# Two scores before the last block of queries: a barrier removed at the start of a banded attention

## The reference, cut to what matters

```python
p = h @ w_in
q, k, v, mq = jnp.split(p, [Q_W, Q_W + KV_W, Q_W + 2 * KV_W], axis=-1)
...
scores = jnp.einsum('bnqhgd,bnkhd->bnhgqk', qb, kb) * (ATTN_HEAD_DIM ** -0.5)
scores = jnp.where(mask, scores, NEG)            # |key - query| <= 128
m = jnp.maximum(jnp.max(scores, axis=-1, keepdims=True), s)   # s: a sink for each head
p = jnp.exp(scores - m)
probs = p / (jnp.sum(p, axis=-1, keepdims=True) + jnp.exp(s - m))
out = jnp.einsum('bnhgqk,bnkhd->bnqhgd', probs.astype(v.dtype), vb)
...
mo = memory_attention(mq, mk, mv)
x = x + jnp.concatenate([mixed, mo], axis=-1) @ w_out[l]
```

## Time and profile before

| | |
|---|---|
| median of 3 runs | 3200.7 us (3200.01 to 3201.22) |
| the profiled execution | 3196.59 us |
| its span, first to last instruction | 3194.8 us |
| mean granted TensorE clock | 0.989 |
| TensorE, busy | 3080.3 us, 96% |
| VectorE, busy | 1696.2 us, 53% |
| ScalarE, busy | 1105.6 us, 35% |
| GpSimd, busy | 89.9 us, 3% |

### The profile page before, as it was taken

One profiled execution on the slowest core, in us unless ns is written; L12 is line 12 of the kernel. 1 busy time (PEld: TensorE's weight loads), 2 busy tenths in 40 slices (PEclk: granted clock), 3 DMA queues, 4 the chain that ended last, 5 costly groups with the idle time before them and its releaser, 6 DMA issues. The chain is left out here.

```text
span 3194.8 us, 34615 instructions
## 1 busy us (share of the span) xinstructions
PE 3080.3 (96%) x14262; PEld 2387.1 (75%) x14272; DVE 1696.2 (53%) x2173; ACT 1105.6 (35%) x1723; POOL 89.9 (3%) x70
## 2 busy tenths in 40 slices
PE   8999999999999999999999999999999999999888
PEld 7885567788888888777777888888887687666566
DVE  7737854544444433589854633333333734656575
ACT  4215632311111111387732311111111515776552
POOL 0004510000000000000000000000000000000000
PEclk9999999999999999999999999999999999999999
DMA  4320011122222211211131111111111131000213
GB/s 148 114 94 1 1 73 34 53 80 66 67 79 73 73 47 47 86 47 47 54 124 34 47 47 46 47 53 46 47 47 46 53 124 35 20 21 20 93 39 121
DMA packets 54510, 190.96 MB, mean 60 GB/s; under 512 B 6288, under 2 KB 6672, under 8 KB 54224
## 3 DMA queue, kind: packets, MB, share of 16 engines
q1 hardware_dynamic: 54352, 188.74, 18.0%
HBM read 172.73 MB, written 14.68 MB: 59 GB/s over the span
## 5 line engine op out<-in xcount | busy, mean ns | idle before, releaser
L285 PE MATMUL PS<-H,wsp 128*128 128x512 f32 x6864 | 1613.8, 394 | 38.7 <-DVE wsp L141 16.5
L285 PEld LDWEIGHTS PS<-H,wsp 128*128 128x128 f32 x6864 | 1290.6, 189 | 347.1 <-issue 40.1
L285 PE MATMUL PS<-p,wsp 128*128 128x512 f32 (+1 forms) x3840 | 895.2, 393 | 20.7 <-DVE p L141 20.7
L285 PEld LDWEIGHTS PS<-p,wsp 128*128 128x128 f32 x3840 | 711.3, 189 | 198.6 <-ACT wsp L138 21.5
L138 ACT ACTIVATE p<-p 128x1024 f32<-128x1024 f32 (+7 forms) x426 | 361.3, 872 | 861.6 <-DVE p L144 678.6
L138 ACT ACTIVATE wsp<-raw 128x1024 fp32r<-128x1024 f32 (+1 forms) x267 | 276.9, 1040 | 698.3 <-PE PS L285 490.9
L141 DVE TENSOR_TENSOR p<-p,PS 128x1024 f32<-128x1024 f32 (+2 forms) x232 | 244.4, 1054 | 496.5 <-PE PS L285 496.5
L141 DVE TENSOR_TENSOR wsp<-raw,wsp 128x1024 fp32r<-128x1024 f32 (+1 forms) x267 | 321.8, 1207 | 159.4 <-ACT wsp L138 152.4
L141 DVE TENSOR_TENSOR p<-PS,p 128x1024 f32<-128x1024 f32 (+2 forms) x116 | 131.0, 1130 | 371.8 <-PE PS L285 346.9
L141 DVE TENSOR_TENSOR p<-p 128x1024 fp32r<-128x1024 f32 (+5 forms) x239 | 239.6, 1010 | 114.8 <-ACT p L138 111.6
L285 PE MATMUL PS<-p 128*64 128x256 f32 (+9 forms) x1432 | 283.9, 464 | 12.7 <-ACT p L138 3.0
(11 more groups left out here) (70 smaller groups left out, 1051.4 us busy)
## 6 DMA issues: line engine op xcount, KB each, us to landing
raw<-in_in_dram SPq DMA_DIRECT2D x72, 512.0 KB, 3.5
raw<-in_dn_dram SPq DMA_DIRECT2D x65, 512.0 KB, 3.5
raw<-in_up_dram SPq DMA_DIRECT2D x64, 512.0 KB, 3.5
raw<-in_out_dram SPq DMA_DIRECT2D x42, 512.0 KB, 3.5
p<-in_ada_dram SPq DMA_DIRECT2D x24, 512.0 KB, 4.4
p<-in_x_dram SPq DMA_DIRECT2D x16, 512.0 KB, 7.3
raw<-in_kv_dram SPq DMA_DIRECT2D x16, 512.0 KB, 3.5
spill_dram<-p SPq DMA_DIRECT2D x16, 512.0 KB, 2.9
```

Of the source, the lines that this page charges most:

```text
L285: return pe(lambda e: e.matmul(o, l, r, start=start, stop=stop, **kw), *a)
```

## The change

The project call makes three blocks of memory queries in place of four. The fourth becomes a function `last_queries`, handed to `attention_units` as `lead`, which calls it after the second score group of unit 0 has been put into the lists; it sets the counter to 2 for it, so that it takes banks 4 and 5. The barrier is gone. In its place the scores and the values wait for the last operations of ScalarE, VectorE and GpSimd as they stood behind the third block (`heads_done`), the first users of `Pb` and of the transposed buffers wait for the same, and the second `Pb` buffer waits for the fourth block's eviction as well.

```diff
         def attention_units(units, nkmax, off, scale, sink=None, fill=None, fills=(), early=False, ahead=None, wide=None,
-                            pt_wait=None):
+                            pt_wait=None, lead=None):
...
-            pt_free, p_free = [pt_wait] * nT, [None, None]
+            pt_free, p_free = [pt_wait] * nT, [pt_wait, None]
...
                     pending = x
+                    if lead and u == 0 and j == J - 1:
+                        o = lead()
+                        p_free[1] = [*(pt_wait or ()), o]
                     for _ in range(fills[u] if fill and early else int(bool(fill) and fills[u] > 1)):
...
-        project("in0", 4, 8, Hk, by_R(MQ, R, box["r"], *kv_done))
-        Q.barrier()
+        project("in0", 3, 8, Hk, by_R(MQ, R, box["r"], *kv_done))
+
+        stage_end = heads_done = [x for x in (Q.last("act"), Q.last("dve"), Q.last("pool")) if x]
+
+        def last_queries():
+            pair[0] = 2
+            project("in0", 1, 8, Hk, lambda n, *a: by_R(MQ, R, box["r"], *kv_done)(3, *a))
+            return Q.last("dve")
...
-        attention_units(window_units(Qt, Kt, Vt, 2, 4, (-1, 0, 1), out0, bias0, sinkv0), 384, 80 * KB, 0.125, True)
+        attention_units(window_units(Qt, Kt, Vt, 2, 4, (-1, 0, 1), out0, bias0, sinkv0, heads_done, heads_done), 384, 80 * KB, 0.125, True,
+                        pt_wait=stage_end, lead=last_queries)
```

## The result

The changed kernel takes 3193.6 us (median of 12 runs, 3188.3 to 3194.6), the kernel before in the same session 3198.7 us (median of 12, 3192.3 to 3201.2). The ratio is 0.9982, with a 95% interval of 0.9973 to 0.9990: a gain of 0.18%, which is 5.8 us by the ratio, 5.2 us by the medians. The prediction had 3.8 us (0.12%), gave "no difference" 0.89, and put the forecast time 3.3 us above the measured one. The direction and the three places were right. The term of the start was mis-sized by more than its own length: 2.1 us expected, 4.97 in the two profiles.

What follows compares the result with a forecast made beforehand. TensorE, busy 96% of the span, was taken to bound the kernel. Start 2.1, first seam -1.2 and second seam 2.9 sum to 3.8 us, so 3200.7 becomes 3196.9 us; range 3193.0 to 3201.8.

Steps and rivals of the forecast that it cites:

- The term of the start: Start of the first banded attention: unit 2's second group turned at 261.95 instead of 264.06, a gain of 2.1 us.
- The wait in front of the scores: Before the first scores: the 1.48 us wait on an eviction stays, one block earlier, so scores start at 234.27.
- The fall of the clock over the held-back block: Over the held-back block's 48 matmuls: one 3.41 us stretch of half clock, costing 1.7 us.
- The rival that I gave 0.17: Clock stays up at the held-back block: start gains 3.8 us, whole gain 5.5 us, 3195.2 us; chance 0.17.
- The order on VectorE behind the block: Unit 0's second normalisation queues behind the block's eviction and unit 1's first maximum; its turn comes 3.8 us after eviction start.
- The pace behind it: First attention units behind the held-back block: two units take 9.6 us at full clock.
- What comes along: Weight split and 512 KB load accompanying the held-back block: hidden under its matmuls, cost nothing; uncovered some 2.4 us.
- The first seam: Rest of the first output projection: shifted bank pairs make a block wait for bank 7's eviction, loss 1.2 us.
- The second seam: Last output projection: shifted bank pairs remove its first block's 2.93 us idle wait for bank 7, gain 2.9 us.
- the rival without a fall: Clock stays at full rate at the held-back block: gain 5.5 us, giving 3195.2 us; chance 0.17.
- The noise: Whole-kernel timing: a measurement tells 0.2%, 6.4 us, from no change; "same" given 0.89.
- the rival of a second fall: Behind the held-back block the clock falls again, two units keep 11.51 us: gain 1.9 us, 3198.8 us; chance 0.16.

Runs made afterwards that it cites:

- Early waits: Changed kernel, but scores, values and first probabilities wait for the last operations before the first memory-query block, not behind the third; median 3190.4 us, ratio 0.9975 to the kernel before.
- before again: The unchanged kernel before, profiled a second time for its clock; one execution, 3196.6 us.
- the barrier alone: Kernel before without its barrier, four blocks and nothing moved, attention waiting for the last operations behind the fourth block; median 3196.5 us, ratio 0.9993.
- the first try without a gap: Kernel before without barrier, four blocks in pairs 0, 1, 2, 3, scores not waiting for these blocks, nothing held back; median 3200.7 us, ratio 1.0005.
- the rotation alone: Kernel before with four blocks and its barrier, but the bank-pair counter set to 3 behind the first attention; median 3195.5 us, ratio 0.9990.
- the second seam alone: Kernel before with one line more, the bank-pair counter set to 1 in front of the last output projection; median 3196.5 us, ratio 0.9983.

## Why the prediction was right or wrong

*The wait in front of the scores.* Right: it stays, 1.36 us, and belongs to the eviction. Early waits remove it.

*The fall of the clock over the held-back block.* Wrong, and it is the step that failed: "I don't think it does: what comes before the block is the same as what came before the fall." What came before was the same, what came after was not. In seven profiles with work held back (the changed kernel twice and five kernels made from it) the clock fell over the block in none; in two it fell behind it, for 3.4 us. In the seven with nothing held back it fell in the first units every time, for 3.4 to 13.7 us. The block's eviction started 46.8 us behind the mark, where the working has 46.7 without the fall and 48.4 with it. The rival that I gave 0.17 was the case. Without the fall, the term's own working (E + 13.4 for unit 2's second turn) gives 3.8 us. The length of 3.41 us that I took for the fall rested on a single stretch as well: near 1290 it was 3.4 us long in four of the 14 profiles, 6.8 in five and 10.2 in five.

What in the held-back work keeps the clock up stays open. The block does two things at once, it puts dense matmuls behind the scores and takes the wait for unit 0's exponentials away from TensorE, and no run has one without the other. Nor do the waits behind the block decide: they are the same 1.5 us in six of these seven profiles (0.56 and 0.96), and the clock fell there in two of the six.

*The order on VectorE behind the block.* Right to a tenth: unit 0's second group is turned 251.25 - 247.44 = 3.81 us after the eviction's start, 3.8 expected; the waits are 0.56 and 0.96 us, 0.6 and 0.9 expected.

*The pace behind it.* Mis-sized: I took 9.6 us for two units from the end of the attention, they take 8.4 at the start. That is another 1.2 us, and 3.8 + 1.2 = 5.0 is what was measured (4.97). The two pieces are not of the same shape after all. Inside the 9.59 us the eviction of a finished output stands on ScalarE and VectorE in front of the copies out of the turn's banks, and TensorE waits 0.65 and 0.34 us for these, 0.23 and 0.16 us later on; in the 8.38 us at the start no output is finished yet, and its waits are 0.27 and 0.25. These waits differ by 0.9 us of the 1.2; no run tests it. The row in the profile of before:

```profile
416.14 0.41 PE L538 MATMUL PS<-cf,p 128*128 128x128 f32 x2 [0.65 <-ACT p L138]
```

With a fall behind the block I took the old pace, 11.5 us, for two units; measured with a stretch of 3.4 us, 258.89 - 249.43 = 9.46.

*How much was the old clock?* The kernel before is not one case. With a stretch of 13.7 us unit 2's second turn comes at 64, with 3.4 or 6.8 us at 61.8 (in two kernels that are the same up to there); the changed kernel has it at 59 or 60. So the start gives 1.8 to 5.4 us, by the execution. I had read one profile of before as the kernel's fixed state.

*What comes along.* Right: the split is done at 240.9 under the block, and no wait for the load behind it shows on TensorE. The barrier's own price is 0.2 us of TensorE's time, and taking it out without moving anything makes no difference that the timing can tell.

*The first seam.* Right: 1.2 us expected, 1.04 measured, undone in each of the three kernels with the counter taken back.

*The second seam.* Right in the profile: 2.9 expected, 3.0 measured, and a version with that line alone keeps it. Too small as an expectation for a median: a fall of the clock followed the idle time there in three of the six profiles that have the gap (before again, the barrier alone, the first try without a gap), 1.4 us more each time (84.5 to 84.8 from there to the end, against 83.1), and in none of the eight that don't have it.

*The sum.* In the two profiles the three places give 6.9 us where the sum has 3.8: the start is 2.9 us better than its term, the seams together 0.3. The timing, 5.2 to 5.8 us, lies at the 5.5 of the rival without a fall, and that is partly luck: the rival's term for the start, 3.8 us, left out the faster pace, and the two profiles compare a start of before with a long fall to one of after with none, which is nearly the most that the four profiles of the two kernels allow (5.4 us).

*The noise.* Wrong, the second step that failed: "A measurement of this kernel tells 0.2%, 6.4 us, from no change", and with it the 0.89 for "no difference". The bound had no run or row behind it. Twelve runs of each kernel gave an interval of 0.9973 to 0.9990, 0.09% to either side, so a gain of 0.18%, inside my bound, can be told from none.

*The rule on transposes.* Part 4 of the Trainium skill's page "TensorE: Matmul & The Clock Gate" says that they do not count as activity like matmuls; by that rule the rival of a second fall would have been the case. It came in two of seven profiles, right where the first turns are, and cost 1.1 us there. So the trace agrees in part.

## What to carry to other kernels

Where a phase of dense matmuls is followed by one of short ones that starts with a chain over other engines, keep back a dense piece that doesn't depend on the chain and lay it behind the chain's first links; half a block was enough here. It paid twice, in the wait that it covered and in the clock, which fell in the first units of every profile without it and, for 3.4 us, in two of seven with it. A counter that deals out banks is part of the timing: before it is moved by an edit, list the places where rotating users follow fixed ones, and set it there on purpose; one such line was worth 3.0 us in the profile, the whole change 6.9. And take more than one profile of before where its clock is not at 1.00: a stretch of low clock may be 3.4 or 13.7 us long in the same program.

## What the runs showed of the hardware

*How long the low clock lasts.* With the same code up to there, its length in the first units was 13.7, 13.7, 6.8, 3.4 us (before twice, the rotation alone, the second seam alone). In the short, waiting work of these units TensorE stayed at 1.2 GHz while the records show it busy 12.46 of 13.65 us; but dense work is no warrant of a short stretch either: near 1290, in the midst of the MLP, it was 3.4, 6.8 or 10.2 us long.

```profile
243.75:246.10 2.35, 1.77 (x12) 1.00 0.00 0
246.10:259.75 13.65, 12.46 (x50) 0.50 0.00 1
```

*A fall in dense work.* Every profile has one near 1290 (1283 to 1295), where TensorE is shown busy without a break before it. I have no cause for it. It is the only one of its kind: each profile has 9 to 13 other stretches of low clock, and shortly before every one of those TensorE had been idle for 1.5 us or more in all. Idle time of that size did not always bring a fall, as the second seam and the end of the attention show.

*The first 200 us.* The mark comes at 198.4 to 199.0 us in the executions whose clock did not fall near 90, and at 200.1 to 201.0 in those where it did, for 3.4 us. Half of it would be 1.7 us, so this fall would account for nearly all of the distance between two classes of starts, which is as wide as the effects of this study.
